# Grid attention cut into column tiles, with the low parts of queries and keys subtracted on GpSimd

## The reference, cut to what matters

```python
C_KH, C_KW, C_HEADS, GRID_W = 8, 16, 16, 64
def neighbourhood_latent(q, k, v, kc, vc, rpb):
    cs = jnp.clip(col - C_KW // 2, 0, GRID_W - C_KW)
    col_ok = (col[None, :] >= cs[:, None]) & (col[None, :] < cs[:, None] + C_KW)
    ...
    s_loc = einsum(qr, kr) * scale + bias          # bias from rpb, by row and column distance
    s_loc = jnp.where(mask, s_loc, -jnp.inf)       # mask: col_ok for every row
    s_ctx = einsum(qr, kc) * scale
    p = jax.nn.softmax(jnp.concatenate([s_loc, s_ctx], axis=-1), axis=-1)
    return p_loc @ vr + p_ctx @ vc
y = (o * jax.nn.silu(z)) @ out_w
```

## Time and profile before

| | us |
|---|---|
| median of 3 runs | 2283.3 (2283.01 to 2284.41) |
| span of the profiled execution | 2281.6 |
| TensorE busy | 2230.1 (98%) |
| VectorE busy | 1283.6 (56%) |
| ScalarE busy | 925.7 (41%) |
| GpSimd busy | 280.3 (12%) |

### The profile page before, as it was taken

How to read it: one execution, slowest core, us unless ns; L and a number is a source line. 1 busy time by engine, 2 the same in 40 slices (tenths; PEclk the granted TensorE clock), 3 DMA queues, 4 the chain that set the end, 5 groups by cost and what they waited for, 6 DMA issues and landing times.

```text
span 2281.6 us, 33000 instructions
## 1 busy us (share of the span) xinstructions
PE 2230.1 (98%) x13479; PEld 1852.9 (81%) x13479; DVE 1283.6 (56%) x1884; ACT 925.7 (41%) x1558; POOL 280.3 (12%) x175
## 2 busy tenths in 40 slices
PE   7999999999999999999999999999999999999998
PEld 7876688888888776788888888888888888888887
DVE  4687548964225778459853235414667462225884
ACT  3447743222214347742222223224655342124773
POOL 2001322121332002222111000000100000000000
PEclk9999999999999999999999999999999999999999
DMA  5220025632893210035532421221000214212221
GB/s 161 88 70 2 1 94 181 202 114 75 209 266 89 77 56 1 20 129 185 166 111 75 143 88 48 83 79 42 19 18 16 78 62 164 74 56 75 69 66 56
DMA packets 149417, 205.80 MB, mean 90 GB/s; under 512 B 42485, under 2 KB 95746, under 8 KB 149250
## 3 DMA queue, kind: packets, MB, share of 16 engines
q1 hardware_dynamic: 110288, 169.83, 22.9%
q10 hardware_dynamic: 38914, 33.69, 5.7%
q0 software_dynamic: 64, 0.16, 0.0%
HBM read 188.85 MB, written 14.82 MB: 89 GB/s over the span
## 4 chain that ended last, share of the span: by engine, by line
PE 91%; DVE 4%; ACT 3%; issue 2%; DMA 0%; ACTq 0%; POOLq 0%; DVEq 0%
PE ps L526 68%; PE ps L1858 4%; PE ps L1892 3%; PE ps L2509 3%; PE ps L1909 2%; PE ps L2526 2%; PE ps L2538 2%; DVE probs_t L2116 1%; PE ps L2514 1%; PE ps L733 1%; ACT probs_t L2615 1%; DVE neg_max L2060 1%; PE ps L533 1%; PE ps L2512 1%; PE ps L2546 1%
## 5 line engine op out<-in xcount | busy, mean ns | idle before, releaser
L491 DVE TENSOR_TENSOR w_low<-w_raw,w_high 128x2048 fp32r<-128x2048 f32 (+4 forms) x140 | 303.5, 2168 | 491.6 <-ACT w_high L486 491.4
L486 ACT ACTIVATE w_high<-w_raw 128x2048 fp32r<-128x2048 f32 (+4 forms) x140 | 253.0, 1807 | 602.0 <-PE ps L526 549.9
L526 PE MATMUL ps<-h_hi,w_high 128*128 128x512 f32 (+1 forms) x1168 | 439.6, 376 | 1.2 <-DVE w_low L491 0.6
L526 PE MATMUL ps<-h_lo,w_high 128*128 128x512 f32 (+1 forms) x1168 | 437.3, 374 | 0.0
L526 PE MATMUL ps<-h_hi,w_low 128*128 128x512 f32 (+1 forms) x1168 | 436.9, 374 | 0.0
L526 PEld LDWEIGHTS ps<-h_hi,w_high 128*128 128x128 f32 x1168 | 220.0, 188 | 42.1 <-DVE w_low L491 1.2
L526 PEld LDWEIGHTS ps<-h_hi,w_low 128*128 128x128 f32 x1168 | 219.8, 188 | 39.6
L526 PEld LDWEIGHTS ps<-h_lo,w_high 128*128 128x128 f32 x1168 | 220.0, 188 | 39.3 <-issue 0.5
L526 PE MATMUL ps<-w_high,h_hi 128*128 128x512 f32 (+3 forms) x576 | 214.0, 372 | 0.6 <-DVE h_lo L2906 0.6
L526 PE MATMUL ps<-w_low,h_hi 128*128 128x512 f32 (+3 forms) x576 | 211.6, 367 | 0.0
L526 PE MATMUL ps<-w_high,h_lo 128*128 128x512 f32 (+3 forms) x576 | 211.4, 367 | 0.0
(11 more groups left out here) (372 smaller groups left out, 3869.8 us busy)
## 6 DMA issues: line engine op xcount, KB each, us to landing
w_raw<-in_w_gate_up SPq DMA_DIRECT2D x44, 1024.0 KB, 5.2
ada_w<-in_ada_w SPq DMA_DIRECT2D x24, 1024.0 KB, 5.2
w_raw<-in_w_down SPq DMA_DIRECT2D x20, 1024.0 KB, 5.3
w_raw<-in_w_in SPq DMA_DIRECT2D x16, 1024.0 KB, 5.1
w_raw<-in_c_in_w SPq DMA_DIRECT2D x16, 1024.0 KB, 5.4
w_raw<-in_w_out SPq DMA_DIRECT2D x8, 1024.0 KB, 5.0
w_raw<-in_ab_in_w SPq DMA_DIRECT2D x8, 1024.0 KB, 5.2
mask_table<-bias_scratch ACTq DMA_DIRECT2D x32, 224.0 KB, 7.6
```

The lines of the kernel that those rows point to most:

```text
L486: e.activation(w_high[j % 2][:, 0:size], w_raw[j % 2][:, 0:size], ACT.Copy).then_inc(sig.w_high_done, 1)
L491: e.tensor_tensor(w_low[j % 2][:, 0:size], w_raw[j % 2][:, 0:size], w_high[j % 2][:, 0:size].bitcast(F32), ALU.subtract).then_inc(sig.w_lo ...
L526: mm = e.matmul(dst, lhs, rhs, start=start and a == 0, stop=stop and a == 2)
```

## The change

The grid stage is written anew as `GridPairs`. The queries of the grid are ordered by columns: block 0 holds columns 0 to 7 and 56 to 63, blocks 1 to 3 hold 16 columns each, of all 8 rows; keys and values are ordered in four blocks of 16 columns. A query block then needs two key blocks of 128, not four. A step scores 256 grid keys and 256 context keys (12 matmuls of 256 columns), has 8 transposes and 16 value matmuls. Scores have three buffers of 2 banks, and the work is issued one step further ahead: in iteration s TensorE issues `turn_probs(s)`, `scores(s + 2)`, `values(s - 1)`. VectorE's `tensor_tensor_reduce` per head, its negation and the separate context maximum become one add over both heads and one negated maximum over 1024 columns. VectorE copies head 0's turned probabilities, ScalarE head 1's (512 columns each). `pair_low` is issued by GpSimd. `copy_o` and `gate_wide` put the result back in token order, each in two instructions, and `copy_o(u)` stands at the head of ScalarE's iteration 4u + 5. Elsewhere: the bias table has [2, 2, 256] columns a pair and not [2, 14, 64], loaded by 8 DMAs of 16 partitions and masked by four adds; `mod_full` of the grid tokens is written by four instructions of 128 columns; the queries are copied out by three instructions a bank; two small DMAs at the start become four.

```diff
+            LOWS_ON_POOL = True
+                self.cut_at = {4 * p - 6 + c: (p, c) for p in range(1, U) for c in range(2)}
...
+                    here = slice(b - 1, b + 1) if b else slice(0, 4, 3)
+                    for c, blocks in enumerate((here, slice(4, 6))):
+                        for n in range(3):
+                            for m in range(2):
...
+                                mm = e.matmul(dst, q, k, start=n == 0, stop=n == 2)
...
+                    if b == 0 and u:
+                        e.wait_ge(sig.o_done, B["o_done"] + u)
...
+                for s in range(self.N + 1):
+                    if s < self.N:
+                        turn_probs(s)
+                    if s == 1:
+                        keep_warm(e, 6, 3)
+                    if 1 <= s < self.N - 2:
+                        scores(s + 2)
+                    if s % 4 == 3:
+                        wide(s // 4)
+                    if s >= 1:
+                        values(s - 1)
...
+                for s in range(-2, self.N + 1):
+                    if s % 4 == 1 and s >= 5:
+                        copy_o(s // 4 - 1)
+                    if 0 <= s < self.N:
+                        copy_second(s)
+                    if s + 2 < self.N:
+                        exps(s + 2)
...
+                    if s in self.cut_at:
+                        p, c = self.cut_at[s]
+                        if p >= 2:
+                            e.wait_ge(sig.scores_ready, B["scores_ready"] + 4 * p - 4)
+                        pair_high(e, p, c)
...
+                    ch.step(e.tensor_tensor(here, here, bias2[u % 2][:, min(b, 1), :, :], ALU.add))
+                    ch.wait(e)
+                    e.tensor_reduce(out=neg_max2[:, 2 * s:2 * s + 2], in_=self.both(s), op=ALU.max, axis=AX.X,
+                                    negate=True).then_inc(sig.max_ready, 1)
...
+                for s in range(-2, self.N + 1):
+                    if 0 <= s < self.N:
+                        copy_first(s)
+                    if s % 4 == 0 and s >= 4:
+                        gate_wide(s // 4 - 1)
+                    if s + 2 < self.N:
+                        maxima(s + 2)
...
+                    if s % 4 == 2 and s > 0:
+                        invert(s // 4)
...
+            def gpsimd(self, e, B, L, ch):
+                def lows(p):
+                    for c in range(2):
+                        pair_low(e, B, p, c, 2 * p - 1 + c)
+
+                if self.LOWS_ON_POOL:
+                    lows(1)
+                    lows(2)
+                for u in range(self.U):
+                    e.wait_ge(sig.wide_ready, B["wide_ready"] + u + 1)
+                    e.wait_ge(sig.o_done, B["o_done"] + u + 1)
+                    e.tensor_tensor(o_all3[:, u, :], o_raw2[:], wide2[:], ALU.mult).then_inc(sig.o_scaled, 1)
+                    if self.LOWS_ON_POOL and 3 <= u + 3 < self.U:
+                        lows(u + 3)
...
+                        if self.l and v == 0:
+                            cuts = [(by_blocks(dst)[:, :, j], by_rows(x)[:, :, j], by_rows(inv)[:, :, j]) for j in range(4)]
...
-                    for m in range(2):
-                        for half in range(2):
-                            e.dma_start(mask_tables[n % 4][64 * half:64 * half + 64, m, :, :], bias_source(2 * n + m, half)).then_inc(sems[f"bias_raw{n % 2}"], 16)
+                    for w in range(8):
+                        e.dma_start(bias_raws[n % 4][16 * w:16 * w + 16], bias_source(n, w)).then_inc(sems[f"bias_raw{n % 2}"], 16)
```

More of the change, by code:

```diff
@@ L105, in shape_tables @@
     put("before", np.where(j >= i, 0, NEG))
[L106 to L109, removed]
+    seen = np.zeros((16, 2, 2, 16), bool)
+    cell, key = np.arange(16)[:, None], np.arange(32).reshape(1, 2, 16)
+    seen[:, 0] = (cell < 8)[:, :, None] == (key >= 16)
+    seen[:, 1] = (key >= cell[:, :, None]) & (key < cell[:, :, None] + 16)
+    put("colmask", np.tile(np.where(seen[::-1], 0, NEG).reshape(16, 64), (8, 1)))
     pos = np.arange(S, dtype=np.float32)
@@ L1658, in invert_wide, with __init__ @@
                 self.invert(e, B, inv_wide[:])
-        def backwards(a):
-            return a.rearrange("p (r c) -> p r c", c=64)[:, :, ::-1]
         class Split(Stage):
[L1667 to L1670, removed]
+            def __init__(self, src, hi, lo, first=0, cut=None):
+                self.src, self.hi, self.lo = ((lambda k, a=a: a[:, k, :]) for a in (src, hi, lo))
                 self.first, self.cut = first, cut
@@ L1757, in __init__ @@
                         prior = ("qk_ready" if event[0] == "turn" else "wide_ready", event[1] + 1)
-                self.cut_at = {4 * p - 5 + c: (p, c) for p in range(1, U) for c in range(2)} if grid else {}
                 T = len(turns)
-                self.counts = {"qk_bank": T, "qk_ready": T + len(self.cut_at), "scores_ready": N, "half_scored": sum(map(bool, self.paired)), "max_ready": N,
+                self.counts = {"qk_bank": T, "qk_ready": T, "scores_ready": N, "half_scored": sum(map(bool, self.paired)), "max_ready": N,
                                "probs_ready": 2 * N, "probs_turned": 2 * N, "turned_ready": N, "turned_second": sum(self.rest), "o_ready": N,
                                "o_done": U, "inverse_wide": U, "wide_ready": U, "o_scaled": U, "staged_ready": U,
[L1763 to L1769, removed]
+                               "qk_high": T, "z_load0": 16 * U, "sink_ready": self.sinks, "sink_exp": self.sinks,
+                               "part_high": 4, "part_low": 4, "keys_staged": 1, "rope_staged": 1}
             def unit(self, s):
@@ L1778, in spread @@
             def spread(self, u):
-                there = not self.grid and u % 2
+                there = u % 2
                 return (wide_there if there else wide2)[:, 0:self.units[u].cols], (z_there if there else z_unit)[:, 0:self.units[u].cols]
@@ L1921, in tensor @@
                     turn(i, i)
-                if not self.grid:
-                    keep_warm(e, 6, 4)
+                keep_warm(e, 6, 4)
                 for s in range(-1, self.N + 1):
@@ L1929, in tensor @@
                     if s == 0:
-                        keep_warm(e, 6, 10 if self.grid else 5)
+                        keep_warm(e, 6, 5)
                     if 0 <= s < self.N:
@@ L1935, in tensor @@
                         turn(i, 7)
-                    if s - 1 in self.ends and (self.grid or s < self.N):
+                    if s - 1 in self.ends and s < self.N:
                         wide(self.ends[s - 1])
@@ L1942, in tensor @@
                         turn(i, 7)
-                if not self.grid:
-                    wide(self.ends[self.N - 1])
+                wide(self.ends[self.N - 1])
             def scalar(self, e, B, L, ch):
@@ L1961, in exps @@
                     n, tiles = self.keys(s), len(self.steps[s][1])
[L1962 to L1963 removed]
+                    e.wait_ge(sig.max_ready, B["max_ready"] + s + 1)
                     if s >= 2:
@@ L2013, in scalar @@
                 load_z(0)
-                if not self.grid:
-                    load_z(1)
-                if self.grid:
-                    load_bias(1)
+                load_z(1)
                 for s in range(-1, self.N + 1):
@@ L2044, in scalar @@
                         sink_exp(self.ends[s + 1])
-                    if not self.grid and self.N - 6 <= s < self.N - 2:
+                    if self.N - 6 <= s < self.N - 2:
                         high_part(s - self.N + 6)
```

323 lines of the change are left out of this document (206 added, 117 removed).

## The result

The changed kernel takes 2251.9 us (median of 4 runs, 2251.5 to 2252.0); the kernel before took 2283.3 beside it. The ratio is 0.986, 95% interval 0.9846 to 0.9874. The profiled execution spans 2250.0 us, where 2281.6 was before. Single executions of a kernel can be 2 to 4 us longer, and in the three such executions that were profiled TensorE's granted clock falls for 20 to 40 us long before the grid stage (0.83 from 260 to 280 us in one, 0.86 and 0.87 from 940 to 960 us in the other two). TensorE is still the engine that sets the time.

What follows compares the result with a forecast made beforehand. TensorE, busy 98% of the span, was taken as the bound, VectorE close behind. Grid stage 109.2 for 144.5 (-35.3), mod_full +2.0, last copy_o +0.1: -33.2, so 2283.3 becomes 2250.1 us; range 2238 to 2262.

Steps and rivals of the forecast that it cites:

- A step of 2.82 us: TensorE in the grid stage: transposes 0.97, values 0.97 and scores 0.88 us; four steps with the inverse 11.72, before 17.5.
- The 0.44 for the inverse: TensorE in the grid stage: transposing the spread inverse costs 0.44 us once a pair, 8 x 0.44 = 3.5 in all.
- Scores at 0.88: TensorE, grid step: 12 score matmuls of 256 columns take 0.88 us, from a window-attention row, bounds 0.80 and 1.34.
- rival (b): Grid-stage scores keep the old price of 1.34 us a step: +11 us, time 2261; chance 0.10.
- The order wait, seven times 1.67: At 7 pair ends TensorE's values(4u + 4) wait 1.67 us for ScalarE's copy_o(u); with restarts 12.5 us given back.
- The start at 3.0: Start of the grid stage: 3.0 us extra, from first transposes' wait 1.2, second head 0.2, rounding 0.8, warming and copy 0.7.
- mod_full +2.0: VectorE, before the weights' low part: four 128-column instructions a chunk cost +0.34 each for six chunks, +2.0 us (+0.8 to +2.5).
- The last copy_o +0.1: End of the grid stage: the last output copy as two instructions adds 0.1 us.
- The low parts on GpSimd at 0: Grid stage: moving low-part subtractions from VectorE to GpSimd costs 0 (bound 0 to 0.5), covered by 3 us of slack.
- Rival (a): The order wait at pair ends doesn't bind as ScalarE gets ahead: stage 96.7 us, time 2237.6; chance 0.11.
- Rival (c): GpSimd's low parts come late in the grid stage through contention: some 14 us at most, time 2264; chance 0.06.
- Rival (d): Grid-stage gaps of 1.7 us pull TensorE's clock to 1.2 GHz: stage 190 us, time 2331; chance 0.03.

Runs made afterwards that it cites:

- The run with seven moved inverses: Against the early copy: for seven pairs the inverse's transposes go directly ahead of the next turning of probabilities, the last pair's stay; 2242.3 us.
- the early copy: Against the changed kernel: ScalarE issues a pair's output copy in iteration 4u + 4, ahead of the exponentials of step 4u + 6, not behind them; 2243.7 us.
- the kernel with three more products: Against the changed kernel: GpSimd does three more products of the same width (with ones, changing nothing) ahead of each low-part subtraction; 2289.2 us.

## Why the prediction was right, and where it wasn't

The forecast was 2250.1 and the result is 2251.9. By its steps:

- **A step of 2.82 us.** It is 2.95, so this term was mis-sized. I divided 1.46 us by the number of matmuls. But 12 transposes take 1.46 and 8 take 1.02, 24 value matmuls 1.46 and 16 take 1.02: that is 0.11 and 0.055 a matmul, and 0.14 for each group that follows another kind of work, which a shorter group doesn't save. The 0.44 for the inverse was read where it stood behind other transposes; behind scores it is 0.59. TensorE's work in a round is 12.47 us (13.69 less the wait of 1.22, the restart included) for my 11.72. Eight rounds make +6.0, of which 0.6 is the restart behind each wait, which I had put with the wait. The run with seven moved inverses shows the fixed part by itself.
- **Scores at 0.88.** They are 0.91. The row of the same shape was the right one, and rival (b) with 1.34 is out.
- **The order wait, seven times 1.67.** The place, the count and the releaser were right: the early copy took all of it away. It is 1.22 us each. The chain from the end of the scores (2117.61) to the values (2121.78) is 4.17 us for my 4.5: gate_wide ends at 2117.66, so it was all but out of the way (0.05 for my 0.17 + 0.22), and two instructions of the output copy take 0.55, not 0.66 + 0.1. Against that the way back to TensorE takes 0.14 for my 0.04, and maximum and exponentials some 0.1 more. TensorE had 2.95 us of its own to do in that time, for 2.82. Seven times 1.78 less 1.22 is -3.9.
- The two misses cancel in part, and that is mostly luck. A TensorE that needs longer for its steps waits less for the others, which is 7 x 0.13 = 0.9 of the 3.9, and 0.7 of it is the restart, counted with the steps here. The other 2.3 come from a chain that was shorter for reasons of its own. With the start, +6.0 - 3.9 - 0.3 = +1.8, the stage's 111.0 for 109.2.
- **The start at 3.0.** 111.0 less seven rounds of 13.69 and one of 12.47 leaves 2.7. (The four parts that I had named add up to 2.9.)
- **mod_full +2.0.** It is +2.0 in the trace (from the start of the last matmuls ahead, 1857.29 and 1857.32, to the product: 16.7 us became 18.7), and -2.1 when it is uncut.
- **The last copy_o +0.1.** From the last values to the output product it took 4.4 us before and 4.2 after, so -0.2; what was at stake is as small as that. The stage, mod_full and this add up to -31.8; the span lost 31.6.
- **The low parts on GpSimd at 0.** Their durations, 1.27 and 1.82, and the slack of 3.6 us were right, and one more product before each hardly matters. The sentence that they "can't gain on TensorE's path before VectorE is the bound" was wrong. They spare 2.3 us of the stretch with VectorE at 89% of the stage, as, by the rows above, their place in VectorE's queue lies on the chain of the order wait. The old kernel gives 0 for the same move. The total was not touched by this, since I compared with a VectorE that has no low parts; but the credit of the named edit is 2.3 of the 33.9 us that the stretch lost, and the new tiling has the rest, with its third buffer of scores and its order of work, which no run took apart.
- **Rival (a)**, the wait doesn't bind: what it describes is the early copy, which gives 2243.7 and not 2237.6. Of the 6.1 between them the step of 2.95 is 32 x 0.13 = 4.2 and the inverse of 0.59 another 8 x 0.15 = 1.2; 0.7 stays open.
- **Rival (c)**, GpSimd late: not in this kernel. It takes between two and four times its work to bring it about at more than one pair. The contention that the rival names exists, but the other way round: it is VectorE's subtraction that grew, from 0.95 to 1.85, and GpSimd's product stayed at 1.28.
- **Rival (d)**, the clock: 1.00 all through the stage, with seven waits of 1.22 us. The mechanism is real in the kernel with three more products, where waits of 1.22 and 2.00 us stand close together. Where between the two it sets in was not tried. That the trace before bore it out nowhere was wrong, though. Ahead of the last layer's products, behind a wait of 0.8 us and twelve matmuls of one column, it has this window:

```profile
1855.00:1860.00 5.00, 4.90 (x22) 4.43 (x22) 1.96 (x5) 0.92 (x3) 0.00 (x0) 0.66 0.00 0
```

The changed kernel shows the same 0.66 there, and the run with mod_full uncut 1.00 behind the same wait. What decides between the two was not tried, so that the seven waits of the stage leave the clock alone is measured, and was not to be had from the trace before.
- The Trainium skill (GPSIMD Engine Reference, Engine selection) puts elementwise work of two inputs on VectorE. The factor of 2 holds (1.82 for 0.95), but the conclusion doesn't hold here: what counts is which engine has room when the work is due. Its remark (Key points) that the two engines share their way into SBUF, with contention where VectorE has two SBUF inputs, is borne out in one place, 1.85 us for 0.95 on VectorE, with the product on GpSimd unchanged at 1.28.

## What to carry to other kernels

An engine with spare time can still lengthen a wait: ask of each small instruction whether it stands in the queue ahead of one that the longest chain goes through, and move the awaited copy forward before anything is moved to another engine. Price a group of matmuls as a fixed part and a part for each, from two groups of different size, and put groups of one kind next to each other. When medians of two kernels differ by less than a disturbance elsewhere in the program, compare the stretch of the trace in which they differ.

## What the runs showed of the hardware

- A group of transposes or of value matmuls on TensorE carries a fixed 0.14 to 0.15 us when it follows another kind: 12, 8 and 4 transposes took 1.46, 1.02 and 0.59 us so, 8 and 4 took 0.87 and 0.44 behind other transposes.
- A VectorE subtraction of two SBUF operands took 0.95 us alone and 1.85 beside a GpSimd product of two SBUF operands, which itself stayed at 1.28 and had begun 0.25 us earlier; held apart, it was 0.95 again in 7 of 7. VectorE's copies and additions that read PSUM kept their 0.69 and 0.70 in the changed kernel, where GpSimd was busy 30.6 of 111 us.
- GpSimd's subtraction of 768 columns took 1.82 us and of 512 columns 1.27, whether the tiling before or after ran beside it.
- Seven single waits of 1.22 us, 13.7 us apart, left TensorE's clock at 1.00; in the kernel with three more products, waits of 1.22 and 2.00 us some 3 us apart were followed by 0.65, and over that stage, at 0.87, the same matmuls took 116.67 us for 101.57. Elsewhere a wait of 0.8 us was followed by 0.66 in some executions and by 1.00 in others.
